# High and low halves of the activations laid side by side, word by word, in a two-block transformer kernel

## The chip, the cores and the metric

The kernel runs on one core of a Trainium2 chip. A time is the device time of one execution in microseconds (us), and a kernel's time is the median of its runs. A profile is one further execution, recorded instruction by instruction. Its span runs from the first to the last instruction of the core.

## The reference, cut to what matters

The reference is a transformer stack in float32 with 256 tokens and a model width of 1,024: a block with an RWKV mixer and an attention mixer, then a block with forgetting attention, then one with a state-space mixer (S5). Each block ends in a feed-forward part with 2,816 hidden columns. For this change only one thing in it matters: nearly all of the work is products of an activation (256 rows) with a large weight.

```python
proj = h @ w_in[l]                                   # 256 x 1024 by 1024 x 5408
x = x + (g_a * u_a + g_b * u_b) @ w_out[l]
return (jax.nn.gelu(a, approximate=False) * b) @ w_down      # 256 x 2816 by 2816 x 1024
return (jax.nn.silu(h @ w_gate) * (h @ w_up)) @ w_down
```

## The kernel before, in words

**Three products for one.** A float32 number is split into a high half, rounded to the format fp32r that TensorE takes in one pass, and a low half, the rest. Each product is then high by high, low by high and high by low, added up in PSUM. The weights are streamed from memory in slabs of 128 x 1024 words (`raw`). ScalarE rounds a slab to `whi` (line 1420), VectorE subtracts to get `wlo` (line 1817), and TensorE takes both as its moving operand, up to 512 columns at a time.

**The activations stand.** An activation is first turned by TensorE, 128 x 128 at a time, so that its columns lie on partitions (`turn_pair`, line 2668). ScalarE then writes the high half from PSUM (lines 1428, 1432, 1441, 1613, 1630, 1761 and 1771) and VectorE the low half, which reads the high half back (lines 1825, 1830, 1839, 2123, 2168, 2451 and 2461). The halves lie in two tensors of their own: `a_hi` and `a_lo`, 8 tiles of 128 x 256 each, for what is 1,024 columns wide, and `f0`, `f1`, `f2` (shown in the trace as `f_hi`, `f_lo`), 22 tiles each, for the three hidden layers. A product loads 128 columns of one tile as its standing operand:

```python
xh, xl = (a[:, k0 + k, j * P:(j + 1) * P] for a in t.acts[acts])
```

There are 1,288 such products in the program, thus 3,864 pairs of a weight load and a matmul. 48 of these have 288 moving columns, the others 512.

**One place takes them the other way round.** `forget_mm` (lines 3021 to 3023, 24 matmuls) loads a small weight as the standing operand and streams 256 columns of the activation halves as the moving one.

**What sets the order.** A host-side list (`order_of_work`) holds all parts of the work in one order, and each engine's program walks through it and takes its own parts. Waits are on semaphores whose values are counted from marks in the same list, not from memory addresses. So where a tensor lies does not enter the order.

**Memory under other memory.** The tensor `over` (11,264 words a partition) lies on the same addresses as `f1`. It holds tables of the S5 mixer: `cp`, `cp3`, `near` and the turned input `uT`. Some of them are filled while the last products that read `f1` are still to come.

Of the kernel before, what the change touches and what calls it, by code (L numbers as in the profile page):

```python
# [10 lines left out]
F32R = mybir.dt.float32r  # L11
# [4 lines left out]
P = 128  # L16
S = 256
# [1110 lines left out]
def place(nc, ctx):  # L1128
    t = Tiles()

    def sb(name, shape, dt=F32, stack=ctx):
        return stack.enter_context(nc.sbuf_tensor(name, shape, dt))
# [6 lines left out]
    t.whi = [sb(f"whi{i}", [P, 1024], F32R) for i in range(NH)]  # L1139
    t.x = sb("x", [P, 2, D])  # L1140
    t.h = sb("h", [P, 2, D])
    a_hi, a_lo = sb("a_hi", [P, 8, S], F32R), sb("a_lo", [P, 8, S], F32R)
    t.con = sb("con", [P, NCON])
    t.maskw = sb("maskw", [P, 3 * P], mybir.dt.int16)
    t.maskb = t.maskw[:, :].bitcast(BF16).rearrange("p (a s) -> p a s", a=3)
# [64 lines left out]
        t.ua = [view(52 + 2 * i, 512) for i in range(4)]  # L1210

    def hidden(name, stack):
        t.acts[name] = (sb(name + "_hi", [P, 22, S], F32R, stack), sb(name + "_lo", [P, 22, S], F32R, stack))

    with ExitStack() as s3:
        hidden("f0", s3)
        t.at = [sb(f"at{i}", [P, 2, 512], F32, s3) for i in range(2)]
        t.aT = [sb(f"aT{i}", [P, 2, S], F32, s3) for i in range(2)]
        t.cv = [sb(f"cv{i}", [P, 2, S], F32, s3) for i in range(2)]
# [22 lines left out]
    with ExitStack() as s6:  # L1242
        rot = sb("rot", [P, 4096], F32, s6)
        t.ct, t.stb = (rot[:, 2048 * i:2048 * i + 2048].rearrange("p (i j) -> p i j", i=32) for i in range(2))
        t.tmp512 = [rot[:, 512 * i:512 * i + 512] for i in range(4)]
        t.tmp1024 = [rot[:, 1024 * i:1024 * i + 1024].rearrange("p (k g) -> p k g", k=8) for i in range(4)]
        t.pr = sb("pr", [P, 16, 32], F32, s6)
        t.bt = [sb(f"bt{i}", [P, 8, 2, P], F32, s6) for i in range(4)]
        rdc = sb("rdc", [P, 1024], F32, s6)
        t.rd = [rdc[:, 512 * i:512 * i + 512] for i in range(2)]  # L1250
        old = CON_AT["bones"]
        t.cc = [sb("cc0", [P, 32, 2, 16], F32, s6)] + [a.rearrange("p (i r c) -> p i r c", i=32, r=2) for a in (t.con[:, old:old + 1024], rdc[:, :])]
        t.bT = [a.rearrange("p (k r c) -> p k r c", k=2, r=2) for a in (t.con[:, old + 1024:old + 1536], t.sqj[:, :])]
        t.eye4 = t.con[:, old + 1536:old + 1568]
        t.skip = t.con[:, old + 1568:old + 1824].rearrange("p (k c) -> p k c", k=8)
        with ExitStack() as s5:
            hidden("f1", s5)
        over = sb("over", [P, 11264], F32, s6)
        t.cp = [over[:, c0:c0 + 3072].rearrange("p (i r k c) -> p i r k c", i=16, r=2, k=3) for c0 in (0, 5632)]
        t.cp3 = over[:, 3072:5120].rearrange("p (i r c) -> p i r c", i=32, r=2)  # L1260
        t.near = [over[:, c0:c0 + 384].rearrange("p (k d c) -> p k d c", k=4, d=3) for c0 in (5120, 10752)]
        t.uT = over[:, 8704:10752].rearrange("p (k s) -> p k s", k=8)
    with ExitStack() as s5:
        hidden("f2", s5)
# [1893 lines left out]
def program(nc, A, out):  # L3158
    with ExitStack() as ctx:
        s = Signals(lambda name: ctx.enter_context(nc.semaphore(name)))  # L3160
        t = place(nc, ctx)
        order = order_of_work()
        m = Marks()
# [162 lines left out]
```

## Time and profile before

| what | value |
|---|---|
| median of 3 runs | 1154.11 us (1153.53 to 1157.0) |
| the profiled execution's own time | 1152.62 us |
| its span | 1150.8 us, 18422 instructions |
| TensorE matmul | 1102.9 us busy, 96% |
| TensorE weight load | 910.4 us busy, 79% |
| VectorE | 783.4 us busy, 68% |
| ScalarE | 598.0 us busy, 52% |
| GpSimd | 119.6 us busy, 10% |
| granted TensorE clock | 0.996 of full speed |

Busy time of TensorE (PE) counts each matmul from its start to its modelled end, and these overlap; how fast the engine goes is seen from the distance between two starts in the timeline. PEld is the row of weight loads, which run beside the matmuls. DVE is VectorE, ACT is ScalarE, POOL is GpSimd.

### The profile page before, as it was taken

The numbers are of one execution on the slowest core, as the hardware profiler recorded it, in microseconds if no ns is written. First come the engines' busy times: TensorE is split into PE (matmuls) and PEld (weight loads), VectorE is DVE, ScalarE is ACT, GpSimd is POOL, SyncE is SP. The second block draws the span as 40 slices with busy tenths as digits, with TensorE's granted clock in tenths as the row PEclk, the third lists the DMA queues.
The fourth block names the chain that finished last, engine by engine and source line by source line (L and its number), as shares of the span: only waits on it lengthen the run. The fifth ranks groups of instructions, "written<-read, shape, count | busy, mean of one in ns | idle before, by whom it ended". The sixth has DMA issues, their size and how long they took to land.

```text
span 1150.8 us, 18422 instructions
## 1 busy us (share of the span) xinstructions
PE 1102.9 (96%) x7620; PEld 910.4 (79%) x7620; DVE 783.4 (68%) x1268; ACT 598.0 (52%) x927; POOL 119.6 (10%) x122
## 2 busy tenths in 40 slices
PE   7999999999999999999998999999999799999997
PEld 6777878777888888887877887878878688888786
DVE  6747874767677775658566896887578867555553
ACT  6566533243665663565655654445672267345441
POOL 0405050500000000000000000012105400000000
PEclk9999999999999999999999999999999999999999
DMA  8533322024654555555323654555531245555551
GB/s 316 183 115 121 129 75 75 21 74 146 200 184 165 183 178 189 183 166 192 122 90 110 255 185 151 182 198 190 175 130 58 76 165 183 189 180 190 192 200 57
DMA packets 49668, 177.50 MB, mean 154 GB/s; under 512 B 5648, under 2 KB 6288, under 8 KB 49328
## 3 DMA queue, kind: packets, MB, share of 16 engines
q1 hardware_dynamic: 49440, 175.79, 45.0%
q8 instruction: 60, 0.98, 0.4%
q10 hardware_dynamic: 144, 0.52, 0.1%
q14 instruction: 24, 0.20, 0.1%
HBM read 175.25 MB, written 1.05 MB: 153 GB/s over the span
## 4 chain that ended last, share of the span: by engine, by line
PE 79%; DVE 12%; ACT 6%; issue 2%; POOL 1%; DMA 0%; SPq 0%; DVEq 0%; ACTq 0%
PE wps L2679 22%; PE wps L2681 21%; PE wps L2680 21%; PE tps L2668 4%; DVE wlo L1817 3%; ACT whi L1420 1%; PE wps L3123 1%; PE tps L2909 1%; DVE arena L2039 1%; PE tps L2914 1%; PE tps L2725 1%; DVE bt L2434 1%; PE tps L3089 1%; DVE bt L2445 1%; PE tps L2886 1%
## 5 line engine op out<-in xcount | busy, mean ns | idle before, releaser
L1817 DVE TENSOR_TENSOR wlo<-raw,whi 128x1024 fp32r<-128x1024 f32 (+1 forms) x322 | 390.4, 1232 | 174.1 <-ACT whi L1420 172.7
L2679 PE MATMUL wps<-whi,a_hi 128*128 128x512 f32 (+1 forms) x1008 | 400.5, 397 | 4.6 <-DVE a_lo L1825 2.3
L2681 PE MATMUL wps<-wlo,a_hi 128*128 128x512 f32 (+1 forms) x1008 | 391.9, 389 | 0.0
L2680 PE MATMUL wps<-whi,a_lo 128*128 128x512 f32 (+1 forms) x1008 | 391.1, 388 | 0.0
L1420 ACT ACTIVATE whi<-raw 128x1024 fp32r<-128x1024 f32 (+1 forms) x322 | 327.2, 1053 | 76.2 <-PE wps L2681 76.1
L2679 PEld LDWEIGHTS wps<-whi,a_hi 128*128 128x128 f32 x1008 | 189.3, 188 | 45.7 <-issue 5.9
L2681 PEld LDWEIGHTS wps<-wlo,a_hi 128*128 128x128 f32 x1008 | 189.2, 188 | 40.1
L2680 PEld LDWEIGHTS wps<-whi,a_lo 128*128 128x128 f32 x1008 | 189.6, 188 | 36.8 <-issue 0.5
L2679 PE MATMUL wps<-whi,f_hi 128*128 128x512 f32 x264 | 103.3, 391 | 0.0
L2681 PE MATMUL wps<-wlo,f_hi 128*128 128x512 f32 x264 | 102.8, 389 | 0.0
L2680 PE MATMUL wps<-whi,f_lo 128*128 128x512 f32 x264 | 102.7, 389 | 0.0
L2681 PEld LDWEIGHTS wps<-wlo,f_hi 128*128 128x128 f32 x264 | 49.6, 188 | 10.3
L2679 PEld LDWEIGHTS wps<-whi,f_hi 128*128 128x128 f32 x264 | 49.6, 188 | 10.2
L2680 PEld LDWEIGHTS wps<-whi,f_lo 128*128 128x128 f32 x264 | 49.6, 188 | 10.1
L1428 ACT ACTIVATE f_hi<-tps 128x512 fp32r<-128x512 f32 x22 | 12.1, 596 | 71.7 <-PE tps L2668 71.7
L1441 ACT ACTIVATE a_hi<-tps,vec 128x128 fp32r<-128x128 f32 x72 | 19.7, 381 | 28.7 <-PE tps L2668 28.7
L2619 POOL TENSOR_TENSOR rot<-pr,con 128x512 f32<-128x512 f32 x4 | 6.1, 1516 | 268.9 <-DVE bt L2372 268.9
L1455 ACT ACTIVATE h<-wps,st 128x512 f32<-128x512 f32 (+1 forms) x28 | 17.9, 658 | 30.2 <-PE wps L2681 30.0
L1455 ACT ACTIVATE at<-wps,st 128x512 f32<-128x512 f32 x22 | 15.0, 690 | 32.8 <-PE wps L2681 31.3
L1825 DVE TENSOR_TENSOR f_lo<-tps,f_hi 128x512 fp32r<-128x512 f32 x22 | 14.3, 686 | 25.5 <-ACT f_hi L1428 25.5
L2212 DVE SCALAR_TENSOR_TENSOR h<-wps,st,h 128x512 f32<-128x512 f32 (+1 forms) x24 | 16.1, 703 | 21.7 <-PE wps L2681 19.1
L2565 POOL TENSOR_TENSOR arena<-arena,con 128x512 f32<-128x512 f32 x20 | 28.5, 1461 | 0.0
(419 smaller groups left out, 1247.4 us busy)
## 6 DMA issues: line engine op xcount, KB each, us to landing
raw<-in_w_dn SPq DMA_DIRECT2D x22, 512.0 KB, 3.2
raw<-in_w_0dn SPq DMA_DIRECT2D x22, 512.0 KB, 3.2
raw<-in_w_1dn SPq DMA_DIRECT2D x22, 512.0 KB, 3.2
raw<-in_w_ua SPq DMA_DIRECT2D x20, 512.0 KB, 3.2
raw<-in_w_ub SPq DMA_DIRECT2D x20, 512.0 KB, 3.3
raw<-in_w_0ug SPq DMA_DIRECT2D x20, 512.0 KB, 3.3
raw<-in_w_0uu SPq DMA_DIRECT2D x20, 512.0 KB, 3.3
raw<-in_w_1ug SPq DMA_DIRECT2D x20, 512.0 KB, 3.2
```

The source lines that it names most:

```text
L1420: activate(t.whi[n % NH][:, 0:w], t.raw[n % NR][:, 0:w], ACT.Copy).then_inc(m.done(s.act_hi, "hi", n), 1)
L1428: activate(hi[:, k:k + 2, :], by2(t.bank[b][:, :]), ACT.Copy).then_inc(m.done(s.act_out, "hi_of", p, 1), 1)
L1441: activate(hi[:, k, j * P:(j + 1) * P], t.bank[b][:, sub * P:(sub + 1) * P], ACT.Copy, scale=vcol(t, gname, g0 + k)).then_inc(m.done(s.act ...
L1455: activate(t.dst[dst][:, j, c0:c0 + w], t.bank[b][:, 0:w], f, scale=t.st[:, 2 + j:3 + j]).then_inc(m.done(s.act_out, "take", name, j), 1)
L1817: V.tensor_tensor(t.wlo[n % NR][:, 0:w], t.raw[n % NR][:, 0:w], t.whi[n % NH][:, 0:w].bitcast(F32), ALU.subtract).then_inc(m.done(s.dve_lo ...
L1825: V.tensor_tensor(lo[:, k:k + 2, :], by2(t.bank[b][:, :]), hi[:, k:k + 2, :].bitcast(F32), ALU.subtract).then_inc(m.done(s.dve_out, "lo_of ...
L2212: V.scalar_tensor_tensor(d, t.bank[b][:, c0:c0 + w], t.st[:, 2 + j:3 + j], d, ALU.mult, ALU.mult).then_inc(m.done(s.dve_out, "gate_up", up ...
L2565: G.tensor_tensor(t.Ao[l % 2][g], t.Sm[:, hs, 0, :], over4(const(t, "levs", 768)[:, P * l:P * l + P]), ALU.mult).then_inc(m.done(s.pool_ou ...
L2668: return T.transpose(o, i, t.con[0:n, 0:n])
L2679: T.matmul(o, xh, wh, start=first, stop=False)
L2680: T.matmul(o, xl, wh, start=False, stop=False)
L2681: mm = T.matmul(o, xh, wl, start=False, stop=last)
```

## The change

The two halves of an activation become one tensor with a last axis of two: word 2s is the high half of column s, word 2s + 1 the low half. `a_hi` and `a_lo` (and the halves of `f0`, `f1`, `f2`) are now views with a step of two words. 128 columns of a standing operand were 512 adjacent bytes on each partition; they are now every second word of 1,024 bytes. The total size is the same.

Since hidden column tiles of `f1` are now freed in another order of addresses (tile k covers words 512k to 512k + 511, both halves), the tables in `over` are put at other offsets: the second `cp` moves from word 5632 to 3072, `cp3` from 3072 to 6144, the first `near` from 5120 to 8192.

```diff
-    a_hi, a_lo = sb("a_hi", [P, 8, S], F32R), sb("a_lo", [P, 8, S], F32R)
+    pair = sb("a_pair", [P, 8, S, 2], F32R)
+    a_hi, a_lo = (pair[:, :, :, i] for i in range(2))
...
     def hidden(name, stack):
-        t.acts[name] = (sb(name + "_hi", [P, 22, S], F32R, stack), sb(name + "_lo", [P, 22, S], F32R, stack))
+        pair = sb(name + "_pair", [P, 22, S, 2], F32R, stack)
+        t.acts[name] = tuple(pair[:, :, :, i] for i in range(2))
...
-        t.cp = [over[:, c0:c0 + 3072].rearrange("p (i r k c) -> p i r k c", i=16, r=2, k=3) for c0 in (0, 5632)]
-        t.cp3 = over[:, 3072:5120].rearrange("p (i r c) -> p i r c", i=32, r=2)
-        t.near = [over[:, c0:c0 + 384].rearrange("p (k d c) -> p k d c", k=4, d=3) for c0 in (5120, 10752)]
+        t.cp = [over[:, c0:c0 + 3072].rearrange("p (i r k c) -> p i r k c", i=16, r=2, k=3) for c0 in (0, 3072)]
+        t.cp3 = over[:, 6144:8192].rearrange("p (i r c) -> p i r c", i=32, r=2)
+        t.near = [over[:, c0:c0 + 384].rearrange("p (k d c) -> p k d c", k=4, d=3) for c0 in (8192, 10752)]
```

No instruction is added, removed or moved on any engine, and every wait stands where it stood. Only the addresses and the steps of operands differ, and the tensor's name. TensorE's first products before (`wps` is a PSUM bank, `tps` one for turned tiles, `con` the identity):

```order
1 L2668 MATMUL tps<-con,x 128x128 x16
2 L2679 MATMUL wps<-whi,a_hi 128x512
3 L2680 MATMUL wps<-whi,a_lo 128x512
4 L2681 MATMUL wps<-wlo,a_hi 128x512
5 L2679 MATMUL wps<-whi,a_hi 128x512
```

The same place after:

```order
1 L2670 MATMUL tps<-con,x 128x128 x16
2 L2681 MATMUL wps<-whi,a_pair 128x512
3 L2682 MATMUL wps<-whi,a_pair 128x512
4 L2683 MATMUL wps<-wlo,a_pair 128x512
5 L2681 MATMUL wps<-whi,a_pair 128x512
```

Lines behind line 1142 are one further down, and behind line 1213 two further down. 3,864 standing operands, the moving operands of 24 matmuls, 137 ScalarE writes and 137 VectorE operations (which read and write the pair) have the step of two words.

## Rows read from the trace of the kernel before

**Rows 1.** The page: span, busy time of each engine, chain that ended last.

```profile
span 1150.8 us, 18422 instructions
PE 1102.9 (96%) x7620; PEld 910.4 (79%) x7620; DVE 783.4 (68%) x1268; ACT 598.0 (52%) x927; POOL 119.6 (10%) x122
...
PE 79%; DVE 12%; ACT 6%; issue 2%; POOL 1%; DMA 0%; SPq 0%; DVEq 0%; ACTq 0%
```

**Rows 2.** Timeline, TensorE, dense stretch: start us, duration us, engine, line, what.

```profile
1019.67 0.39 PE L2679 MATMUL wps<-whi,a_hi 128*128 128x512 f32 x1
1019.90 0.39 PE L2680 MATMUL wps<-whi,a_lo 128*128 128x512 f32 x1
1019.90 0.19 PEld L2681 LDWEIGHTS wps<-wlo,a_hi 128*128 128x128 f32 x1
...
1021.94 0.39 PE L2680 MATMUL wps<-whi,a_lo 128*128 128x512 f32 x1
```

**Rows 3.** Timeline, TensorE, `forget_mm`: 256 moving columns.

```profile
502.36 0.28 PE L3022 MATMUL tps<-a_lo,wfh 128*128 128x256 f32 x1
502.36 0.19 PEld L3023 LDWEIGHTS tps<-a_hi,wfl 128*128 128x128 f32 x1
...
502.72 0.19 PEld L3023 LDWEIGHTS tps<-a_hi,wfl 128*128 128x128 f32 x1
502.83 0.28 PE L3023 MATMUL tps<-a_hi,wfl 128*128 128x256 f32 x1
```

**Rows 4.** Groups of weight loads: names, shapes, count | busy us, mean ns | idle before.

```profile
L2679 PEld LDWEIGHTS wps<-whi,a_hi 128*128 128x128 f32 x1008 | 189.3, 188 | 45.7 <-issue 5.9 <-DVE wlo L1817 3.5
L2899 PEld LDWEIGHTS tps<-arena 64*64 64x64 f32 x32 | 2.1, 134 | 0.7 <-issue 0.7
L2733 PEld LDWEIGHTS tps<-maskw 128*128 128x128 bf16 x24 | 2.4, 98 | 0.2
```

**Rows 5.** Timeline, TensorE, where products follow turned tiles.

```profile
545.80 0.49 PE L2668 MATMUL tps<-con,fq 128*128 128x128 f32 x3
546.04 0.47 PE L2679 MATMUL wps<-whi,a_hi 128*128 128x512 f32 x1
546.36 0.40 PE L2680 MATMUL wps<-whi,a_lo 128*128 128x512 f32 x1
546.59 0.40 PE L2681 MATMUL wps<-wlo,a_hi 128*128 128x512 f32 x1
```

**Rows 6.** Groups of TensorE: products of 512 and 288 columns.

```profile
L2679 PE MATMUL wps<-whi,a_hi 128*128 128x512 f32 x992 | 395.4, 399 | 4.4 <-DVE a_lo L1825 2.3 <-DVE wlo L1817 1.2 <-issue 0.6
L2680 PE MATMUL wps<-whi,a_lo 128*128 128x288 f32 x16 | 4.7, 295 | 0.0
```

**Rows 7.** Groups of ScalarE: high halves, and reads of PSUM with a step.

```profile
L1428 ACT ACTIVATE f_hi<-tps 128x512 fp32r<-128x512 f32 x22 | 12.1, 596 | 71.7 <-PE tps L2668 71.7
L1432 ACT ACTIVATE a_hi<-tps,vec 128x256 fp32r<-128x256 f32 x12 | 4.8, 485 | 7.2 <-PE tps L2668 7.2
L1441 ACT ACTIVATE a_hi<-tps,vec 128x128 fp32r<-128x128 f32 x72 | 19.7, 381 | 28.7 <-PE tps L2668 28.7
L1758 ACT ACTIVATE over<-wps 128x512 f32<-128x512 f32 x4 | 2.4, 598 | 20.6 <-PE wps L3123 20.6
L1484 ACT ACTIVATE over<-tps 128x512 f32<-128x512 f32 x4 | 2.2, 595 | 3.4 <-PE tps L2668 3.4
```

**Rows 8.** Groups of VectorE: low halves.

```profile
L1825 DVE TENSOR_TENSOR f_lo<-tps,f_hi 128x512 fp32r<-128x512 f32 x22 | 14.3, 686 | 25.5 <-ACT f_hi L1428 25.5
L1830 DVE SCALAR_TENSOR_TENSOR a_lo<-tps,vec,a_hi 128x256 fp32r<-128x256 f32 x12 | 5.1, 478 | 13.0 <-ACT a_hi L1432 13.0
L1839 DVE SCALAR_TENSOR_TENSOR a_lo<-tps,vec,a_hi 128x128 fp32r<-128x128 f32 x72 | 19.5, 344 | 6.2 <-ACT a_hi L1441 5.8
```

**Rows 9.** Span and granted clock of the core.

```profile
core 0: 1150.8 us, clock 0.996
```

## The prediction, made before the changed kernel was run

> **What bounds the kernel now.** I read the page first. TensorE has a matmul under way for 96% of the span, the other engines are at 68%, 52% and 10%, and 79% of the chain that ended last is TensorE's [rows 1]. The reader is to see that only a slower TensorE, or a place where it waits, can move the end. But matmuls overlap, so a busy 96% doesn't say how fast it goes. For that I read the timeline of a dense stretch: each 512-column matmul is shown with 0.39 us, yet from 1019.67 to 1021.94 lie ten starts, thus 0.227 us from one to the next [rows 2]. 3,864 products at that distance are some 877 us (a little less, since 48 are narrower), three quarters of the span. The clock stood at its upper level of 2.4 GHz (0.996 of it over the span) [rows 9], where 512 columns take 213 ns. So the moving operand sets the pace and 14 ns come on top for every matmul.
>
> The weight load is the instruction whose operand the change touches. The timeline shows the load for the next matmul starting with the current matmul and lasting 0.19 us [rows 2]. That 0.19 us isn't its share of the engine, for in `forget_mm` the same kind of load, 188 to 192 ns long, follows the last one after 0.12 us and the matmuls stand 0.117 us apart (502.36 to 502.83 in four steps) [rows 3]. The groups of loads give the same from another side: 128 columns take 188 ns, 64 columns 134 ns [rows 4], so a column costs 54 / 64 = 0.84 ns and the rest, 80 ns, is latency that overlaps. A load holds its path for 128 x 0.84 = 108 ns of the 227 ns between two products. It has 119 ns to spare.
>
> **The change part by part.** No instruction, wait or place in an order changes, so the sum is made of durations alone, and it is the sum of five terms against the profiled execution's own 1152.6 us.
>
> *The 3,816 standing operands of 512-column products.* Each load now reads 128 words out of 1,024 bytes instead of 512. The trace has no load with a step, so I bound it. The best case is 108 ns as now. The nearest row for the price of bytes is the load of the 128-column bf16 tile: 98 ns against 188 ns for twice the bytes [rows 4]. If the price went by the bytes spanned, it would double again, to 216 ns at most. That is still under 227 ns. So at both ends the term is 0, and what hides it is the matmul before it. The cover ends at a load of about 227 ns: from there each further ns costs 3.8 us.
>
> *Loads that nothing covers.* In the program's order a product follows another kind of matmul in 99 places, mostly turned tiles of 128 columns. There the next load is late already: the first product starts at 546.04 and the second only at 546.36, 0.32 us instead of 0.227 [rows 5]. Bounds: 0, and 99 x 0.108 = 10.7 us if the load doubles. I take 0: the nearest rows of an access with a step are two ScalarE reads of PSUM in the S5 part, one taking every fourth word (line 1484) and one every 64th (line 1758). They took 595 and 598 ns, against 596 ns for a read of adjacent words of the same size [rows 7]. A step cost nothing there, though it is another engine and another memory.
>
> The Trainium skill ("Advanced Engine Details and Errata", SBUF Cachelines) says that SBUF has lines of 16 bytes and that two hits on a line are enough for full speed. A step of two float32 words hits each line exactly twice, so by that rule these terms are 0 too; a step of four would break it. No row here shows an SBUF read with a step, and my 0 comes from the bounds above.
>
> *The 48 products of 288 columns* [rows 6]. By 0.417 ns a column and 14 ns on top they stand about 134 ns apart (an estimate from rows 2). Bounds: 0, and 48 x (216 - 134) = 3.9 us. I take 0 as above.
>
> *The 24 matmuls of `forget_mm`.* Here the operand with the step is the moving one, at 2.4 GHz, twice the word rate of a load. Bounds: 0, and 24 x 0.107 = 2.6 us if 256 columns take twice their time. They lie in the open, since TensorE does nothing else there [rows 3]. I take 0, with less faith than elsewhere.
>
> *Writing and reading the halves on ScalarE and VectorE.* 137 operations on each, 39,424 columns in all (72 of 128, 12 of 256, 53 of 512). From 128 to 256 columns ScalarE needs 104 ns more, 0.81 ns a column [rows 7], VectorE 134 ns more, 1.05 ns a column [rows 8]. Both take one column per cycle or slower, so there is no fast mode for adjacent words to lose. Bounds: 0, and 32 us on ScalarE and 41 us on VectorE if a column costs double; against idle shares of 48% and 32% [rows 1] most of it is beside other work. What shows is the way from turned tile to first product at each new activation. The weights' order has 15 of these, and 256 to 512 columns on both engines would add 0.48 to 0.97 us each, 7 to 15 us. I take 0: the PSUM reads with a step are ScalarE's own.
>
> The moved tables in `over` cost nothing: the same tiles are written after the same waits. The sum is 0, or 1152.6 us for a profiled execution. The median of the runs shown lies 1.5 us above that one, so I predict 1154.1 us. Upper ends together: 10.7 + 3.9 + 2.6 + 15 = 32 us.
>
> **The rivals.**
>
> *A load with a step takes twice as long.* For it: the bf16 and float32 loads differ by their bytes [rows 4]. Against it: the stepped PSUM reads, which are free [rows 7]. The place is the 99 uncovered loads, the 288-column products and `forget_mm`: 10.7 + 3.9 + 2.6 = 17.2 us, thus 1171 us, slower than before. It begins to tell from any longer load, since the uncovered ones have no spare.
>
> *The load disturbs the stream.* The 14 ns beyond 213 ns are there on each 512-column matmul, while in `forget_mm` it is 117 - 107 = 10 ns [rows 2, 3]. If they come from the load's reads meeting the stream's, and go by the bytes spanned, they double: 3,864 x 0.014 = 54 us, 1208 us. Against it: a fixed price of changing the standing operand explains them as well.
>
> The Trainium skill ("TensorE: Matmul & The Clock Gate", Part 2, LDWEIGHTS) gives the stationary and the moving operand read ports of their own, which would rule this rival out. The 14 ns show that something is paid per pair, but not what.
>
> *The halves are slower to make.* At 7 to 15 us, say 10, the time is 1164 us. For it: TensorE already waited 2.3 us for `a_lo` [rows 6], so nothing hides this at the starts of a stage. Against it, again, the stepped reads.
>
> *The load passes 227 ns.* At four times 108 ns, 432 ns, each 512-column product waits 0.205 us: 3,816 x 0.205 = 782 us, some 1936 us. Nothing in the rows speaks for it.
>
> *The stream gets better.* If the 14 ns are a clash between the addresses of load and stream and the new layout takes half of it away, the gain is 27 us: 1127 us. Nothing speaks for this beyond the 14 ns.
>
> **How the numbers follow.** About 0.3%, 3.5 us here, is what a measurement of this kernel can tell from no change. Chances: no term at all 0.64; load twice as long 0.15; halves slower 0.09; stream disturbed 0.06; load over 227 ns 0.02; stream better 0.04. So within 0.3% of before 0.63, slower by more 0.32, and faster by more 0.05, with a hundredth moved from the forecast for a measurement that strays. The range is 1150 to 1172 us. The lower end is the forecast less the usual spread; the upper end takes in the slower halves and the doubled load. Left out are the disturbed stream, the two extreme cases and the outer part of the doubled load, together some 0.17.
>
> **What the profile after would show.** Right: the groups of loads at 188 ns, ten starts in 2.27 us in a dense stretch, 0.117 us in `forget_mm`, ScalarE's 512-column halves at 596 ns and VectorE's at 686 ns. A doubled load would show as loads near 295 ns (188 + 107) with the dense stretch unchanged and the second product after turned tiles at 0.43 us. A disturbed stream would show as 0.24 us between starts everywhere. Slower halves would show in their own groups and as TensorE waiting for the low half. The prediction is wrong if any of these moves the median by over 3.5 us, above all if the distance in the dense stretch leaves 0.227 us, for 1 ns there is 3.9 us.

## The result, and the profile after

| | before | after |
|---|---|---|
| median of 4 runs each | 1155.55 us (1153.53 to 1162.31) | 1176.12 us (1175.63 to 1178.93) |
| ratio | | 1.0168, 95% interval 1.0120 to 1.0216 |
| span of the profiled execution | 1150.8 us | 1174.1 us |

Slower by 1.7%, and outside the predicted range of 1150 to 1172 us. The two spans, both at a clock of 0.996, differ by 23.3 us. The page of the kernel after:

```profile
span 1174.1 us, 18422 instructions
PE 1129.8 (96%) x7620; PEld 937.3 (80%) x7620; DVE 784.0 (67%) x1268; ACT 600.5 (51%) x927; POOL 119.7 (10%) x122
...
PE 82%; DVE 10%; ACT 5%; issue 2%; POOL 1%; DMA 0%; SPq 0%; DVEq 0%; ACTq 0%
```

Against [rows 1] TensorE and its loads are busy some 27 us longer, and the rest is almost as it was. The timeline of the same kind of dense stretch as [rows 2]:

```profile
1040.39 0.39 PE L2681 MATMUL wps<-whi,a_pair 128*128 128x512 f32 x1
...
1041.09 0.39 PE L2681 MATMUL wps<-whi,a_pair 128*128 128x512 f32 x1
...
1041.79 0.39 PE L2681 MATMUL wps<-whi,a_pair 128*128 128x512 f32 x1
```

Six starts take 1.40 us, 0.2333 us each, where before ten took 2.27 us, 0.227 each. That is some 6.5 ns more for each of 3,816 matmuls, though the clock and the moving operand are the same. I added up the distances between neighbouring product starts over both traces (3,765 pairs): 862.8 us before, 887.0 us after, 24.2 us more. `forget_mm`, against [rows 3]:

```profile
512.22 0.41 PE L3024 MATMUL tps<-a_pair,wfh 128*128 128x256 f32 x1
512.22 0.21 PEld L3025 LDWEIGHTS tps<-a_pair,wfl 128*128 128x128 f32 x1
...
513.13 0.41 PE L3025 MATMUL tps<-a_pair,wfl 128*128 128x256 f32 x1
```

Four steps take 0.91 us, 0.227 us each in place of 0.117 to 0.120: streaming a moving operand with a step of two words takes twice as long, 24 x 0.107 = 2.6 us. The products and `forget_mm` together are 26.8 us. With both traces laid side by side, matmul by matmul, the other 3.5 us were given back elsewhere, above all where TensorE had waited for another engine for more than 0.7 us: these waits are 4.9 us shorter in sum. The makers of the halves and the loads, against [rows 4], [rows 7] and [rows 8] (the same lines lie one or two further down):

```profile
L2681 PEld LDWEIGHTS wps<-whi,a_pair 128*128 128x128 f32 x1008 | 196.0, 194 | 43.2 <-issue 5.1
L1430 ACT ACTIVATE f_pair<-tps 128x512 fp32r<-128x512 f32 x22 | 12.9, 635 | 74.4 <-PE tps L2670 74.4
L1443 ACT ACTIVATE a_pair<-tps,vec 128x128 fp32r<-128x128 f32 x72 | 19.8, 391 | 29.6 <-PE tps L2670 29.6
L1827 DVE TENSOR_TENSOR f_pair<-tps,f_pair 128x512 fp32r<-128x512 f32 x22 | 14.3, 689 | 29.1 <-ACT f_pair L1430 29.1
```

A load is shown with 194 ns in place of 188. ScalarE writes 512 columns with a step in 635 ns in place of 596, 128 columns in 391 in place of 381. VectorE reads and writes with the step in the same time as before (689 and 686 ns).

### The profile page after: what moved, and what is told of

Read it like the earlier page. It is cut to its first block, busy times and chain, and to the rows that moved or that the text cites. A ratio compares the mean times of both kernels' runs of the same rounds, so it can differ in the third digit from the quotient of the medians.

```text
span 1174.1 us, 18422 instructions
## 1 busy us (share of the span) xinstructions
PE 1129.8 (96%) x7620; PEld 937.3 (80%) x7620; DVE 784.0 (67%) x1268; ACT 600.5 (51%) x927; POOL 119.7 (10%) x122
## 4 chain that ended last, share of the span: by engine, by line
PE 82%; DVE 10%; ACT 5%; issue 2%; POOL 1%; DMA 0%; SPq 0%; DVEq 0%; ACTq 0%
PE wps L2681 22%; PE wps L2682 22%; PE wps L2683 22%; PE tps L2670 5%; DVE wlo L1819 2%; ACT whi L1422 1%; DVE arena L2041 1%; PE tps L2911 1%; PE tps L2916 1%; PE wps L3125 1%; PE tps L2727 1%; DVE bt L2436 1%; PE tps L3091 1%; PE tps L2888 1%; DVE bt L2447 1%
## 5 line engine op out<-in xcount | busy, mean ns | idle before, releaser
L2681 PE MATMUL wps<-whi,a_pair 128*128 128x512 f32 (+1 forms) x1008 | 406.0, 403 | 2.6 <-DVE a_pair L1827 1.5
L2683 PE MATMUL wps<-wlo,a_pair 128*128 128x512 f32 (+1 forms) x1008 | 396.5, 393 | 0.0
L2682 PE MATMUL wps<-whi,a_pair 128*128 128x512 f32 (+1 forms) x1008 | 396.5, 393 | 0.0
L2681 PEld LDWEIGHTS wps<-whi,a_pair 128*128 128x128 f32 x1008 | 196.0, 194 | 43.2 <-issue 5.1
L2683 PEld LDWEIGHTS wps<-wlo,a_pair 128*128 128x128 f32 x1008 | 195.6, 194 | 39.9
L2682 PEld LDWEIGHTS wps<-whi,a_pair 128*128 128x128 f32 x1008 | 195.9, 194 | 36.3 <-issue 0.5
L2681 PE MATMUL wps<-whi,f_pair 128*128 128x512 f32 x264 | 105.4, 399 | 0.0
L2683 PE MATMUL wps<-wlo,f_pair 128*128 128x512 f32 x264 | 104.7, 397 | 0.0
L2682 PE MATMUL wps<-whi,f_pair 128*128 128x512 f32 x264 | 104.4, 395 | 0.0
L2683 PEld LDWEIGHTS wps<-wlo,f_pair 128*128 128x128 f32 x264 | 51.5, 195 | 11.0
L2681 PEld LDWEIGHTS wps<-whi,f_pair 128*128 128x128 f32 x264 | 51.8, 196 | 9.9
L2682 PEld LDWEIGHTS wps<-whi,f_pair 128*128 128x128 f32 x264 | 51.5, 195 | 9.8
L1443 ACT ACTIVATE a_pair<-tps,vec 128x128 fp32r<-128x128 f32 x72 | 19.8, 391 | 29.6 <-PE tps L2670 29.6
L1827 DVE TENSOR_TENSOR f_pair<-tps,f_pair 128x512 fp32r<-128x512 f32 x22 | 14.3, 689 | 29.1 <-ACT f_pair L1430 29.1
```

The costliest lines, as they stand in the source:

```text
L1443: activate(hi[:, k, j * P:(j + 1) * P], t.bank[b][:, sub * P:(sub + 1) * P], ACT.Copy, scale=vcol(t, gname, g0 + k)).then_inc(m.done(s.act ...
L1827: V.tensor_tensor(lo[:, k:k + 2, :], by2(t.bank[b][:, :]), hi[:, k:k + 2, :].bitcast(F32), ALU.subtract).then_inc(m.done(s.dve_out, "lo_of ...
L2681: T.matmul(o, xh, wh, start=first, stop=False)
L2682: T.matmul(o, xl, wh, start=False, stop=False)
L2683: mm = T.matmul(o, xh, wl, start=False, stop=last)
```

## The experiments

In all of them the distance between starts is that of neighbouring product matmuls, as in the timelines. The kernel before has 226.7 ns as its usual distance, which is 213.3 ns of stream at 2.4 GHz and 13.3 ns more; three in a row make 680 ns. The kernel after has 233.3 ns and 700 ns. lo_only, f_only and step0 ran once each, and the kernel before, run beside them, took 1161.0 and 1162.65 us at clocks of 0.986 and 0.984. So their times alone show little, and I go by the distances.

One thing in the trace of the kernel before has to be known for what follows. A product is three matmuls, and when TensorE takes up products again after something else or after a wait, the first two products are often slower than 680 ns, though all their words are adjacent:

```profile
320.07 0.40 PE L2679 MATMUL wps<-whi,a_hi 128*128 128x512 f32 x1
...
320.76 0.40 PE L2679 MATMUL wps<-whi,a_hi 128*128 128x512 f32 x1
...
321.46 0.39 PE L2679 MATMUL wps<-whi,a_hi 128*128 128x512 f32 x1
```

Of the 512-column products followed by another one without a wait, 194 are in first or second place, and 121 of these take 690 to 698 ns; of 879 in a later place only one does.

**hi_only.** Is it the step, or that the halves share 16 bytes? Two tiles of the high half are woven together, the low halves are as before (`Woven` is a view: tile k lies in words k % 2 of pair k // 2). The hidden layers get the same.

```diff
-    a_hi, a_lo = sb("a_hi", [P, 8, S], F32R), sb("a_lo", [P, 8, S], F32R)
+    a_hi, a_lo = Woven(sb("a_hi", [P, 4, S, 2], F32R), 2, 1, 0), sb("a_lo", [P, 8, S], F32R)
```

> The high halves have a step of two words, because two tiles of the high half are woven together; the low halves lie in adjacent words as before, and no word of a low half lies beside a high one. Theory 'stream' (the load of the next standing operand holds up the matmul under way, and more so with a step): the distance from line xh*wh to xl*wh, under which a low half is loaded, stays 227 ns, the two others, under which a high half is loaded, go to 233 ns; two thirds of the loss, some 15 us over before. Theory 'own' (the matmul whose own operand has the step pays): the distance behind xl*wh stays at 227 ns instead. Theory 'sharing' (it costs because both halves lie in the same 16 bytes, written by two engines): all at 227 ns, time as before.

Measured: ratio 1.0163 (1.0093 to 1.0234), a span of 1170.0 us, 19.2 us over before. The stretch at 1002 us:

```profile
1002.15 0.39 PE L2702 MATMUL wps<-whi,a_hi 128*128 128x512 f32 x1
1002.38 0.40 PE L2703 MATMUL wps<-whi,a_lo 128*128 128x512 f32 x1
1002.62 0.39 PE L2704 MATMUL wps<-wlo,a_hi 128*128 128x512 f32 x1
1002.84 0.39 PE L2702 MATMUL wps<-whi,a_hi 128*128 128x512 f32 x1
```

In this stretch the three distances are 231, 236 and 227 ns on average, 693 in all; in other stretches of the same kernel they are 233, 233 and 234, 700 in all, also under the matmul during which a low half without a step is loaded. So sharing is refuted as the cause: no low half lies beside a high one, and 18.9 of the 24.2 us are there. That each distance answers for the one load under it, or for its own operand, is refuted too.

**step4.** Both halves of two tiles are woven, so that a standing operand has a step of four words in the same memory (`woven` makes one tensor whose last axis is four). Of the edit, which is against the kernel after, only the added lines that use it are shown:

```diff
+    a_hi, a_lo = woven(lambda shape: sb("a_pair", shape, F32R), 8, 2)
...
+        t.acts[name] = woven(lambda shape: sb(name + "_pair", shape, F32R, stack), 22, 2)
```

> Two tiles and both halves are woven, so that every standing operand has a step of four words, one per 16 bytes, in the same memory. Theory 'stream', with a price per 16 bytes touched: 32 pieces cost 14 ns over 213 (227), 64 cost 20 (233), so 128 cost 32: 245 ns everywhere, 3,864 x 0.018 = 70 us over before, and forget_mm's stream slower than the 227 ns that a step of two gave. Theory 'load' (the load itself is longer and sets the pace): loads alone grow; with one word per 16 bytes a load takes twice its 108 ns, 216 ns, and the distance is somewhere between 227 and 235 ns. Theory 'any step costs the same': 233 ns, as with two words, 22 us over before.

Measured: ratio 1.0421 (1.0353 to 1.0490), span 1204.9 us. The first line is a group of its loads, the others its timeline, dense and after a turned tile:

```profile
L2704 PEld LDWEIGHTS wps<-wlo,a_pair 128*128 128x128 f32 x1008 | 313.0, 310 | 0.9
```

```profile
1060.52 0.39 PE L2702 MATMUL wps<-whi,a_pair 128*128 128x512 f32 x1
...
1061.92 0.40 PE L2702 MATMUL wps<-whi,a_pair 128*128 128x512 f32 x1
```

```profile
740.04 0.63 PE L2702 MATMUL wps<-whi,a_pair 128*128 128x512 f32 x1
740.51 0.40 PE L2703 MATMUL wps<-whi,a_pair 128*128 128x512 f32 x1
```

Loads last 310 ns instead of 188, the next product after turned tiles starts 0.47 us later instead of 0.32 [rows 5], and the dense distance is 1.40 / 6 = 0.233 here and 235.0 ns on average over the stretches, not 245. A price per 16 bytes touched is refuted. The longer load and the late second product are what I had given for the doubled load, only at a step of four; but the dense stretch isn't unchanged. `forget_mm` streams at 233 ns, hardly slower than with a step of two.

**split_unit, split_step2, split_step4.** What does a load take by itself? Every product is four matmuls of 128 columns with a load each, so that the stream (53 ns) no longer covers the load.

```diff
-        T.matmul(o, xh, wh, start=first, stop=False)
-        T.matmul(o, xl, wh, start=False, stop=False)
-        mm = T.matmul(o, xh, wl, start=False, stop=last)
+        for x_, w_, i in ((xh, wh, 0), (xl, wh, 1), (xh, wl, 2)):
+            for c in range(0, w, P):
+                cols = slice(c, min(c + P, w))
+                mm = T.matmul(o[:, cols], x_, w_[:, cols], start=first and i == 0 and c == 0, stop=last and i == 2 and c + P >= w)
```

> Adjacent words as before, but every product is four matmuls of 128 columns, each with a load of its own: a stream takes 53 ns, a load more, so the distance between starts is the load alone. All theories: 109 ns (as between turned tiles), 15,264 matmuls x 109 ns in place of 3,816 x 227 ns, about 1950 us.

> The same split with the step of two words. Theory 'stream': a load is not longer by itself, 109 ns, time within 5 us of split_unit but for forget_mm's 2.6. Theory 'load': 115 ns, 15,408 x 6 ns = 92 us over split_unit. A load that really takes double: 216 ns, some 1,650 us more.

> A step of four words, matmuls of 128 columns, so the distance is the load alone (it was 112 ns with adjacent words, 118 with a step of two, at full clock). If a load with one word per 16 bytes is what bounds step4, the distance is its 235 ns here too, at full clock. If it is 216 ns or less, step4's 235 is the stream and its handover. If the theory of a price once per load holds for any step, 118 ns.

Measured: 2389.82, 2555.09 and 3964.48 us, one run each. These times can't be compared with each other, for the mean granted clock was 0.873, 0.841 and 0.559. So I read the distances at one level of the clock. TensorE in stretches of 20 us: stretch, length, busy (matmuls), granted clock, DMA share, GB/s; first of split_unit, then of split_step2, then of split_step4.

```profile
1060.00:1080.00 20.00, 20.00 (x182) 1.00 0.31 106
...
1600.00:1620.00 20.00, 20.00 (x96) 0.50 0.16 52
```

```profile
1060.00:1080.00 20.00, 20.00 (x172) 1.00 0.37 110
...
1720.00:1740.00 20.00, 20.00 (x96) 0.50 0.16 53
```

```profile
2500.00:2520.00 20.00, 20.00 (x88) 0.50 0.17 53
```

At 2.4 GHz a load takes 111 ns with adjacent words (median of 11,428 distances) and 118 ns with a step of two (of 10,719). At 1.2 GHz both take 213 ns. With a step of four it is 234 ns at 2.4 GHz (288 of them) and 233 ns at 1.2 GHz (13,881). So the first two go with TensorE's clock, and the third doesn't: there something else is the limit. In step4 the 288-column products, whose stream takes 120 ns, stand 233 ns apart (median; 133 before), so that load sets their pace, and most likely it sets the 235 ns of the 512-column ones too. A step of two costs a bare load 7 ns, as 'load' said. The load is still 109 ns short of 227.

**half_unit, half_step2.** The same edit with matmuls of 256 columns (`range(0, w, 2 * P)`), whose stream and handover, 120 ns, just cover the load.

> Adjacent words, every product in matmuls of 256 columns, each with its own load: the distance that forget_mm showed before, 117 to 120 ns at full clock, so the load (109) is still under the bound of the stream plus its handover (107 + 10 to 13).

> The same with a step of two words. Theory 'once' (every load with a step costs some 6 ns more at the handover, whatever bounds): 124 to 126 ns at full clock, 7,700 loads x 6 = 46 us over half_unit. Theory 'per length' (the stream is held up over its length while the load reads): half of 6, 120 to 123 ns, 23 us over.

Measured: spans of 1199.8 and 1206.5 us at the same clock, 0.988. First half_unit, then half_step2:

```profile
430.00:450.00 20.00, 20.00 (x171) 1.00 0.48 158
700.00:720.00 20.00, 20.00 (x169) 1.00 0.52 182
```

```profile
430.00:450.00 20.00, 20.00 (x171) 1.00 0.48 158
700.00:720.00 20.00, 20.00 (x169) 1.00 0.54 182
```

The median distance is 120 ns in both. Over 7,629 pairs the sum is 927.4 and 929.3 us, 1.9 us for 7,629 loads with a step; the rest of the 6.7 us is `forget_mm` (2.6) and other work. Both forms of the price failed: once per load would be 46 us, by length 23. The 288-column products say the same: 133 ns before, 134 after.

**mix_unit, mix_step2.** From which length on does it cost? The three passes are cut at 384, 448 and 320 columns (pass, cut in the list below, then the rest).

```diff
+        for x_, w_, i, at in ((xh, wh, 0, 384), (xl, wh, 1, 448), (xh, wl, 2, 320)):
+            for c, e in ((0, min(at, w)), (at, w)):
+                if c < e:
+                    mm = T.matmul(o[:, c:e], x_, w_[:, c:e], start=first and i == 0 and c == 0, stop=last and i == 2 and e == w)
```

> Adjacent words; the three passes of a product are cut at 384, 448 and 320 columns, each piece with a load of its own. At 2.4 GHz plus the handover of 13.3 ns the pieces of 384, 448 and 320 columns stand 173, 200 and 147 ns before the next start; pieces of 192, 128 and 64 columns are bound by the load (112 ns).

> The same cuts with a step of two words, under which 256 and 288 columns stayed at 120 and 133 ns while 512 rose from 227 to 233. Theory 'long streams' (the price falls on the part of the stream behind some 288 columns): 320 at 147 to 149, 384 at 173 to 176, 448 at 200 to 205. Theory 'only pieces of a whole bank, 512 columns': 147, 173 and 200 as without a step. Theory 'once per load, hidden in 256 by chance': 153, 180 and 207. Load-bound pieces: 118 ns.

Measured: spans of 1374.6 and 1397.3 us at 0.989 and 0.991. The distances weren't those expected even without a step: behind 384, 448 and 320 columns 205, 258 and 228 ns, behind the rests 58, 28 and 88. With a step they were 204, 265 and 236, and 60, 28 and 87. Per pass of 512 columns that is 263 to 264, 286 to 293 and 316 to 323 ns: nothing for the first, 7 ns for the two others, and the shortest long piece, 320, pays while 384 doesn't. No rule of length comes out, and the run doesn't settle the cause.

**lo_only.** One load in three has the step; the edit is that of hi_only on the low halves.

> Only the low halves have the step of two words (two tiles woven); one load in three. Theory 'each load pays for itself': 1,288 x 6.7 = 8.6 us more span than before plus 0.9 in forget_mm (one of its three streams has the step), 1160 us. Theory 'any load with a step disturbs its neighbours too', as the high halves did with 19 us for two loads in three: 12 to 22 us, 1163 to 1173 us.

Measured: one run, 1171.9 us, span 1170.1 us at a clock of 0.988, so the span holds some loss to the clock as well. By distances:

```profile
1060.48 0.39 PE L2702 MATMUL wps<-whi,a_hi 128*128 128x512 f32 x1
1060.71 0.40 PE L2703 MATMUL wps<-whi,a_lo 128*128 128x512 f32 x1
1060.95 0.39 PE L2704 MATMUL wps<-wlo,a_hi 128*128 128x512 f32 x1
1061.18 0.39 PE L2702 MATMUL wps<-whi,a_hi 128*128 128x512 f32 x1
```

They are 230, 232.4 and 231 ns, 693 for three in nearly all stretches, and the sum over the pairs is 13.5 us above before (876.3 against 862.8). One load in three costs more than half of what all cost (24.2 us), and all three distances grow. 'Each load pays for itself' is refuted; the neighbours are disturbed too. The losses don't add up either: the high halves alone cost 18.9 us and the low ones 13.5, together more than both at once.

**f_only.** A part of the change undone: the 1,024-wide activation lies as before.

```diff
-    pair = sb("a_pair", [P, 8, S, 2], F32R)
-    a_hi, a_lo = (pair[:, :, :, i] for i in range(2))
+    a_hi, a_lo = sb("a_hi", [P, 8, S], F32R), sb("a_lo", [P, 8, S], F32R)
```

> Only the hidden layers (f0, f1, f2) are woven; everything else lies as before, so that a part of the change is undone. If the price falls where the operand has its step and nowhere else: distances of 233 to 238 ns in the 792 matmuls of the three down products and 227 ns in all others, forget_mm at 120 ns; some 6.2 us by the difference between the two traces, a span of 1157 us. If the slower writes of the other halves mattered, less than that would be left for f and the total would not add up to 23 us.

Measured: one run, 1162.76 us, span 1161.0 us, 10.2 us over before. The distances are 233 to 234 ns in the three down products, 227 in all others and 120 in `forget_mm`. Laid beside the trace of before, matmul by matmul, 4.8 us of the 10.2 are lost between 209 and 267 us, where the clock was at its lower level for some 10 us; the other 5.4 us lie in the down products (5.0) and a start 0.4 us later. Windows of f_only, then of the kernel before:

```profile
220.00:240.00 20.00, 18.99 (x267) 0.76 0.01 3
...
1100.00:1120.00 20.00, 20.00 (x87) 1.00 0.56 194
```

```profile
220.00:240.00 20.00, 18.99 (x311) 1.00 0.08 28
...
1100.00:1120.00 20.00, 20.00 (x90) 1.00 0.55 192
```

So the price falls in the stage whose operand has the step and in no other, and 792 matmuls at 6.3 ns are the 5.0 us.

**step0.** The standing operand is one word repeated (`j * P:j * P + 1` broadcast to 128), in the layout of before.

> The standing operand of every product is one word repeated 128 times, so the sums are other numbers than the reference's; nothing else changes. A load touches a single word of 16 bytes. Theory 'per 16 bytes touched' (32 pieces cost 14 ns over the stream, 64 cost 20): the distance falls to some 221 ns, 23 us faster than before. Theory 'a step is what costs, once': a step of zero is handled as adjacent words, 227 ns, or as any step, 233 ns.

Measured: one run, 1163.01 us, span 1161.2 us at 0.994. Loads are shown with 188 to 189 ns, as before, but the distances spread from 224 to 235 ns with a mean of 229.5 (those under 300 ns; 226.4 before), and the sum over the pairs is 873.1 us, 10.3 us above before. 'Per 16 bytes touched' said 221 and is refuted a second time; of the two outcomes named for 'a step costs, once' it is neither. So a pattern with fewer bytes isn't better, and the distance also grows without any step between words: adjacent words are the best of all the patterns tried.

## Why the prediction was wrong, point by point

- **What bounds the kernel:** right. TensorE's stream sets the end, and 1 ns in the dense distance is 3.9 us. This sensitivity was named, and it is what made 6.5 ns into 24 us.
- **The 3,816 standing operands, the step that failed.** I said that "at both ends the term is 0" because the load stays under the matmul before it. The load did stay under it: bare it takes 118 ns, near the best case of my bounds of 108 and 216. But the distance grew by 6.5 ns all the same. f_only shows that it grows in the stages whose standing operands have the step and stays at 227 ns in the others, and hi_only and lo_only that a part of the loads is enough and that the matmuls between them are slowed too. The error was to treat cover as freedom from any effect: at 118 ns a load changed the pace of a stream of 213 ns that covers it. The term was 24.2 us, with the few uncovered loads in it. That the upper ends together, 32 us, would have held the measured loss is luck, for this term had no part in them.
- **Loads that nothing covers, and the 288-column products:** right to take them near 0. 99 x 7 ns would be 0.7 us, measured were 1.2 us over the 99 places (inside the 24.2), and the narrow products moved by 1 ns. The doubling that I had priced at a step of two comes at a step of four.
- **`forget_mm`:** the upper bound was the truth, 2.6 us, and I took 0. ScalarE's free reads of PSUM with a step were a poor guide to TensorE's stream.
- **Making the halves:** ScalarE's part is a little longer, 39,424 columns for 2.5 us more busy time; VectorE's isn't. It doesn't show at the starts of a stage: over the 99 places where a product follows another kind of matmul, the distance to its start is 1.6 us shorter in sum, not longer.
- **The moved tables:** nothing, as said; the S5 stage between 850 and 940 us grew by no more than its products.
- **The rivals.** "The load disturbs the stream" was the right one in kind, at 6% and with 14 ns where 6.5 were measured; its law, price by bytes spanned, is refuted. "A load takes twice as long" (15%) was false for this change.

On the pages I had cited: by the Trainium skill ("Advanced Engine Details and Errata", SBUF Cachelines) two hits on a 16-byte line are enough. The runs agree on where the cliff is for a load: 111, 118 and 234 ns for steps of one, two and four. They don't agree that two hits are free: a bare load pays 7 ns and a moving operand twice its time, 227 ns in place of 120. By the Trainium skill ("TensorE: Matmul & The Clock Gate", Part 2, LDWEIGHTS) the two operands have ports of their own and a load takes no read bandwidth from the running matmul. The stepped loads did slow it; whether at the ports or elsewhere no run here tells.

**What stays open** is the mechanism of the 6.5 ns. Shown is that standing operands with a step bring it on for good, that it isn't the sharing of 16 bytes by the halves, isn't a price per load, per piece touched or by length, and that at 256 and 288 columns it is nearly nothing. It isn't shown that it needs a step: with adjacent words the first two products after a break often take 690 to 698 ns and then settle at 680, and in step0 the distances grow by 3 ns. The distances of three matmuls in a row come out as 680, 693, 700 and 707 ns in different stretches. In five stretches of the kernel after (from 297, 658, 788, 980 and 1105 us) they are 238, 233 and 235 ns with no other difference that I found, which is some 1.8 us of the loss. This looks like two streams of reads that lock into one of a few rhythms, but that is only argued. Block-wise weaving, four words of one half and then four of the other, would have told bytes from lines; it wasn't tried. At a step of two the bytes spanned double as well, and no run tells the one from the other.

## What to carry to other kernels

Keep the 128 words of a standing operand adjacent, and those of a moving operand above all: the first costs 3% of the pace of a 512-column float32 stream at a step of two words, the second doubles its time. When an operation is hidden under another on the same engine, bound its effect on the other's pace too, and multiply by the count before calling it zero. Of all layouts tried the one of the kernel before is the fastest, so nothing here beats it.

## What the runs showed of the hardware that I had not expected

- A load of 128 float32 words takes 111 ns at 2.4 GHz and 213 ns at 1.2 GHz, so it follows TensorE's clock; with a step of four words it takes 233 to 234 ns at either level.
- In the kernels bound by loads the granted clock was low for long stretches though TensorE was busy for 99% of the span: 0.873, 0.841 and 0.559 on average, the lowest where loads take longest. The runs of the kernels with 512-column matmuls had 0.977 to 0.996.
- ScalarE's writes with a step of two words cost 39 ns more for 512 columns (635 against 596); VectorE's cost nothing (689 against 686).
